# Activations transposed between the scatter's two token tiles, bias matmuls of the next item behind the down matmuls

## The reference

```python
def moe_ffn(hn, w_router, b_router, w_gate_up, b_gate_up, w_down, b_down):
    logits = (xt @ w_router + b_router).astype(jnp.float32)
    top_val, top_idx = lax.top_k(logits, TOP_K)
    gates = jax.nn.softmax(top_val, axis=-1)
    ...
    def expert_block(args):
        e, tok = args
        xb = xt[tok]
        gu = xb @ w_gate_up[e] + b_gate_up[e]
        gate, up = jnp.split(gu, 2, axis=-1)
        gate = jnp.minimum(gate, SWIGLU_LIMIT)
        up = jnp.clip(up, -SWIGLU_LIMIT, SWIGLU_LIMIT)
        hmid = (up + 1.0) * (gate * jax.nn.sigmoid(SWIGLU_ALPHA * gate))
        return hmid @ w_down[e] + b_down[e]
    ...
    y = jnp.zeros((t, d), xt.dtype).at[tok_buf].add(out)
```

## Time and profile before

| | |
|---|---|
| median of three runs | 1195.62 us (1194.75 to 1195.65) |
| the profiled execution | 1195.36 us, span 1193.5 us |
| mean granted TensorE clock | 0.994 of full |
| TensorE matmuls busy | 1166.8 us, 98% of the span |
| VectorE, ScalarE busy | 300.0 us (25%), 216.8 us (18%) |
| DMA | 440.28 MB, mean 369 GB/s |
| expert loop on TensorE | 286.8 us to 1182.1 us of the span |

### The profile page before, as it was taken

One profiled execution on the slowest core, in us unless ns is written; L12 is line 12 of the kernel. 1 busy time (PEld: TensorE's weight loads), 2 busy tenths in 40 slices (PEclk: granted clock), 3 DMA queues, 4 the chain that ended last, 5 costly groups with the idle time before them and its releaser, 6 DMA issues.

```text
span 1193.5 us, 14174 instructions
## 1 busy us (share of the span) xinstructions
PE 1166.8 (98%) x5359; PEld 492.6 (41%) x5359; DVE 300.0 (25%) x689; ACT 216.8 (18%) x437; POOL 6.6 (1%) x13
## 2 busy tenths in 40 slices
PE   9999999999999999999999989999999999999996
PEld 4476556854333333333333333333333333333332
DVE  2456553246122111111221111111111121111112
ACT  2120551222111112111111111111111111121112
POOL 0000010000000000000000000000000000000000
PEclk9999999999999999999999998999999999999999
DMA  9800279458999999999999999999999999999994
GB/s 359 367 1 1 100 273 334 164 222 325 397 428 429 428 432 430 431 433 428 435 427 435 427 433 431 430 430 432 432 431 431 429 432 430 424 428 427 428 423 178
DMA packets 31299, 440.28 MB, mean 369 GB/s; under 512 B 4752, under 2 KB 5008, under 8 KB 13872
## 3 DMA queue, kind: packets, MB, share of 16 engines
q1 hardware_dynamic: 30384, 439.32, 87.3%
q10 hardware_dynamic: 864, 0.19, 0.1%
HBM read 438.45 MB, written 1.05 MB: 368 GB/s over the span
## 4 chain that ended last, share of the span: by engine, by line
PE 88%; DMA 8%; DVE 2%; ACT 1%; issue 0%; DVEq 0%; another core or an unknown queue 0%; POOLq 0%; ACTq 0%
PE quad L1570 34%; PE quad L1596 17%; DMA ring<-in_w_gate_up 8%; PE y_banks L1535 5%; PE quad L1519 4%; PE y_banks L1353 2%; PE y_banks L1167 2%; PE quad L1167 2%; PE quad L1527 1%; PE y_banks L1189 1%; PE quad L1545 1%; PE y_banks L1259 1%; PE y_banks L1330 1%; PE quad L1338 1%; PE quad L1464 1%; PE y_banks L1464 1%
## 5 line engine op out<-in xcount | busy, mean ns | idle before, releaser
L1570 PE MATMUL quad<-ring,work 128*64 128x512 f32 x2112 | 465.9, 598 | 7.9 <-DMA ring<-in_w_gate_up 7.7
L1570 PEld LDWEIGHTS quad<-ring,work 128*64 128x64 f32 x2112 | 150.9, 138 | 301.1 <-issue 288.5
L1596 PE MATMUL quad<-ring,work 128*64 128x512 f32 x1056 | 233.9, 594 | 0.3
L1596 PEld LDWEIGHTS quad<-ring,work 128*64 128x64 f32 x1056 | 87.3, 137 | 133.2 <-issue 118.4
L1102 DVE TENSOR_SCALAR work<-quad 128x512 f32<-128x512 f32 x33 | 22.8, 691 | 330.1 <-PE quad L1570 330.1
L644 ACT ACTIVATE work<-work 128x512 f32<-128x512 f32 x33 | 20.8, 630 | 442.4 <-DVE work L1102 442.4
L1021 DVE CAST work<-cst 96x64 bf16 (+1 forms) x34 | 6.5, 191 | 255.2 <-PE quad L1570 255.2
L1535 PE MATMUL y_banks<-work 64*128 64x512 f32 x272 | 67.6, 615 | 0.7 <-ACT work L655 0.7
L1519 PE MATMUL quad<-h,work 128*64 128x512 f32 x272 | 64.2, 593 | 1.6 <-DVE work L1017 1.6
L653 ACT ACTIVATE work<-quad 128x512 f32<-128x512 f32 x33 | 19.7, 597 | 230.2 <-PE quad L1596 230.2
L644 ACT ACT_TABLE_LOAD x33 | 42.3, 1283 | 1.1 <-issue 0.5
(11 more groups left out here) (269 smaller groups left out, 824.9 us busy)
## 6 DMA issues: line engine op xcount, KB each, us to landing
ring<-in_w_gate_up SPq DMA_DIRECT2D x40, 4096.0 KB, 37.0
ring<-in_w_gate_up SPq DMA_DIRECT2D x45, 2048.0 KB, 20.1
ring<-in_w_down SPq DMA_DIRECT2D x20, 4096.0 KB, 35.8
ring<-in_w_down SPq DMA_DIRECT2D x22, 2048.0 KB, 18.4
ring<-in_w_mkv SPq DMA_DIRECT2D x8, 1024.0 KB, 23.1
ring<-in_w_in SPq DMA_DIRECT2D x7, 976.0 KB, 17.4
ring<-in_w_gate_up SPq DMA_DIRECT2D x12, 512.0 KB, 8.8
ring<-in_w_o SPq DMA_DIRECT2D x1, 4096.0 KB, 13.1
```

Source lines behind the costliest of these rows:

```text
L1570: ins = mm(bank[n // 2][lo:lo + BLK, :], xgT[:, k % 4 * P + k // 4 * BLK:k % 4 * P + k // 4 * BLK + BLK], up_rows(j, k)[:, n * 512:(n + 1) ...
L1596: ins = mm(bank[3][n * BLK:(n + 1) * BLK, :], lhs, down_rows(j, f)[:, n * 512:(n + 1) * 512], start=(f == 0), stop=(f == KC - 1))
```

## The change

Only TensorE's order within an item is written anew; no instruction is added or removed.

```diff
                 pe.wait_ge(S["out_copied"], w + 1)
-                scatter().then_inc(S["scattered"], 1)
-                gathered_columns(w + 1)
+                scatter((0,))
+                pe.wait_ge(S["xg_copied"], w + 2)
                 pe.wait_ge(S["hmid_ready"], w + 1)
                 for c in range(4):
                     ins = pe.transpose(bank[2][:, c * P:(c + 1) * P], h_s[:, c * P:(c + 1) * P], ident)
                 ins.then_inc(S["hid_mm"], 1)
-                biases(w + 1)
+                scatter((1,)).then_inc(S["scattered"], 1)
+                gathered_columns(w + 1)
                 pe.wait_ge(S["xg_ready"], w + 3)
                 for f in range(KC):
...
                     if f % (2 * ROWS) == 2 * ROWS - 1:
                         ins.then_inc(S["chunks_used"], 1)
+                biases(w + 1)
                 pe.wait_ge(S["gtok_ready"], w + 1)
```

## The result

The changed kernel takes 1233.32 us in the median of four runs (1232.71 to 1233.73), beside 1195.54 us for the kernel before (four executions): 1.0313 times as long, 95% interval 1.030 to 1.0325, 37.8 us more. The forecast was 1226.7 us, the range 1209 to 1238.

A forecast was written before the change was run, and what follows sets the result against it. TensorE and the loads were taken as nearly level, with 10.53 us of slack. 1195.36 us plus 33 items times 1.27 us (0.82 down matmuls, 0.45 biases), 41.9 us, less 10.5 us slack gave 1226.7 us, range 1209 to 1238.

The forecast's parts named there:

- The bound: Expert loop: TensorE and DMA engines level within 1.2%; all TensorE's slack is 10.53 us of waits for loads.
- the loss at L1631: Low clock at the eight matmuls of 32 rows: assumed to stay; at most 3.5 us less were it gone.
- The activations' transposes: After scatter tile 0, TensorE waits for L1109 until 624.04 and starts these transposes at 624.14; the idle gap is 0.4 us.
- The down matmuls: They start 0.82 us later per item, bounds 0.62 to 1.10, waiting for VectorE's copy L1029.
- nothing is left to cover L1029: Gathered rows' transposes become the last block before the down matmuls, so their 0.69 us copy has no TensorE work beside it.
- the second wait: TensorE's idle gap ahead of the down matmuls, for L1029: 1.0 us in each item.
- the first wait: TensorE's idle gap ahead of the activation transposes, for L1109: 0.4 us in each item.
- The biases: Behind the down matmuls their whole cost is on the path: 0.45 us an item, bounds 0.23 and 0.60.
- The loads: TensorE no longer meets loads; DMA engines stand idle about 8 us once, dipping around 860 to 900 us, at no cost.
- (a): Loads stay the bound: down matmuls start 0.18 us earlier, an item is 0.27 us longer, about 1195.2 us; chance 0.11.
- (b): L1029's cover is partly there: an item costs 0.32 to 0.85 us more, 1196 to 1213 us; chance 0.09.
- (c): Two idle gaps per item make TensorE's clock fall, in one item of three 22 us more, 1249 us; chance 0.07.

The follow-up runs named there:

- the half loads: Only the first chunk of every pair loaded for experts 7 to 26: kernel before 1181.49 us, changed kernel 1233.21 us.
- the third and fourth runs: Kernel before with the scatter split and gathered rows' transposes ahead of the activations': 1195.99 us; the same with biases behind the down matmuls: 1196.17 us.

## Why the prediction was right, point by point

**The bound.** Level engines, 26.54 us of TensorE's against 29.3 of a load, small slack: right, and shown by the half loads. What came off was more than the 10.5 us of waits, since the loss at L1631, which the prediction left in (3.5 us at most), was gone too in the execution profiled: 738.38 to 770.10 is 31.72 us, an item of 28.09 and 3.63 for the eight matmuls, so that of the 33.53 us before 33.53 - 26.54 - 3.63 = 3.4 were low clock. That it was gone is in part chance: in the changed kernel with half loads 1.7 us of it are back.

**The activations' transposes.** Forecast 3.19 us after the gather, measured 3.24, the wait for L1109 0.30 of the 0.4 given.

**The down matmuls.** The step "nothing is left to cover L1029" is right, with the copy's length, its start behind the transposes (0.69 for 0.70) and the second wait (0.97 for 1.0) as they were read. The term was too small, 0.82 instead of 1.12, which is just outside its own bounds of 0.62 to 1.10. Of the missing 0.30, 0.05 is the first wait, 0.12 are the activation transposes and the half scatter behind them (0.56 and 1.06 in place of 0.54 and 0.96), and 0.14 the answer to VectorE: 0.24 us from the end of L1029 to the first down matmul, in place of 0.10; the start of L1029 gives 0.01 back. The 0.24 stood in the earlier trace rows as the upper bound, and 0.20 in the earlier trace rows; the 0.10 was picked below both with no row for it. Half of the 1.92 us of the scatter was too little for half a scatter: two halves take 2.12, and the bounds allowed nothing for that.

**The biases.** Forecast 0.45, measured 0.44, and that their wait costs nothing. The prediction counted them as cover of L1029; the run with them alone moved shows that they were free ahead of the down matmuls, as it assumed.

**The sum.** 33 x 1.56 = 51.5, less 10.5 for the waits and 3.4 for the low clock, gives 37.6; measured 37.8. The forecast was 41.9 less 10.5: two terms off by 9.6 and 3.4 us in ways that partly cancel, so that the total misses by 6.6 us. That much of the closeness is luck; the mechanism is not.

**The loads.** No wait for them any more, and one idle stretch of the DMA engines; forecast about 8 us near 860, found at 850 to 860 with a share of 0.17. The paired loads now land after 12.3 us at least, 22.6 in the median, for 21.7 and 36.5 in the earlier trace rows, as slots come free later.

**The rivals.** (a), the loads as the bound: refuted for this change, but it is what holds in the third and fourth runs, where the item stays at 26.5. (b), cover partly there: no. (c), the clock: the mean granted clock of the changed kernel is 0.999 in the execution profiled and 0.996 to 0.997 in the others, for 0.994 before, with 65 short gaps in the loop, and its items are even at 28.09 us. The swing that the Trainium skill tells of in "TensorE: Matmul & The Clock Gate", section "A second HAM failure mode: psum-queue depth-cycling", does not come with gaps of 0.30 and 0.97 us in 28.09.

## What to carry to other kernels

Before a step is moved up because its result is ready, look at what it was covering: the work that has to be last ahead of a wait should be the work whose follow-up on another engine is shortest or is covered already. Here the two blocks that each release a copy can stand in either order, and the one whose copy is the longer and gates the same matmuls had better go first: that is worth 1.13 us an item with the biases ahead of the down matmuls (27.66 and 26.53) and 1.53 with them behind (28.09 and 26.56). And where two engines are level, count the slack of the loop first (items against loads, and every stretch that is longer than a clean one), for it decides how much of a small cost per item shows in the time.

## What the runs showed of the hardware that was not expected

Waits of TensorE for loads of 2.38 to 2.54 us were followed by a low clock twice and by none twice in one execution (above), so at this length it is not the wait's length alone that decides. The price was 1.69 us in the block behind (8.78 for 7.09) each time.

A low clock also stood right at or behind eight matmuls of 32 rows (L1631) in five of eleven traces, in three of them with no wait for a load anywhere in the loop before it. It cost about 1.7 us in four of them and 3.4 us in one.

Half a scatter, two matmul instructions of 64 rows, takes 1.06 us to the start of the next block, the undivided one with four 1.92: splitting it costs 0.20 us.
